# Six pairs of 21 dot products, a turn in the seventh, and additions at other tiles in a one-core transformer block with retrieved experts

## The reference, cut to what matters

```python
def peer(h, w_peer_q, peer_keys, peer_u, peer_v):
    ...
    idx = jnp.take_along_axis(cidx, fpos, axis=-1)
    g = jax.nn.softmax(fv, axis=-1).astype(h.dtype)
    ...
    def block(args):
        xt, it, gt = args
        u = peer_u[it]
        act = jax.nn.gelu(jnp.einsum('thkd,td->thk', u, xt)) * gt
        return jnp.einsum('thk,thkd->td', act, peer_v[it])
```

## Time and profile before

| | us |
|---|---|
| median of 3 runs | 3876.71 (3874.89 to 3881.01) |
| the profiled execution | 3877.76 |
| its span, first to last instruction | 3876.0 |
| PE busy | 3788.0 (98%) |
| DVE busy | 2360.4 (61%) |
| POOL busy | 1769.0 (46%) |
| PE idle before L1702 with act_hi, ended by DVE w_lo | 42.3 |

### The profile page before, as it was taken

One profiled execution on the slowest core, in us unless ns is written; L12 is line 12 of the kernel. 1 busy time (PEld: TensorE's weight loads), 2 busy tenths in 40 slices (PEclk: granted clock), 3 DMA queues, 4 the chain that ended last, 5 costly groups with the idle time before them and its releaser, 6 DMA issues.

```text
span 3876.0 us, 56148 instructions
## 1 busy us (share of the span) xinstructions
PE 3788.0 (98%) x20205; PEld 3470.2 (90%) x20205; DVE 2360.4 (61%) x3821; ACT 1225.9 (32%) x1418; POOL 1769.0 (46%) x1448
## 2 busy tenths in 40 slices
PE   7999999999999999999999999999999999999998
PEld 5778778888888878899999999999999999999998
DVE  5482552001000228887967787878786777888887
ACT  3433453333333223225632222222222222222121
POOL 0444334444444653442015554555553555555544
PEclk9999999999999999999999999999999999999999
DMA  6223212222222332334579998998998889998887
GB/s 204 88 87 104 70 55 98 97 97 97 97 94 93 139 118 86 110 120 166 206 255 337 338 327 325 330 341 322 331 330 298 299 328 337 336 334 324 326 316 272
DMA packets 212719, 836.78 MB, mean 216 GB/s; under 512 B 21264, under 2 KB 84760, under 8 KB 159256
## 3 DMA queue, kind: packets, MB, share of 16 engines
q1 hardware_dynamic: 124608, 528.52, 38.4%
q0 software_dynamic: 83840, 303.09, 21.3%
q10 hardware_dynamic: 4184, 4.01, 0.5%
HBM read 779.43 MB, written 55.05 MB: 215 GB/s over the span
## 4 chain that ended last, share of the span: by engine, by line
PE 81%; DVE 7%; DMA 6%; issue 4%; ACT 1%; POOL 1%; ACTq 0%; DVEq 0%; POOLq 0%
PE bank L1702 80%; DMA grow<-v_rows,g_col 5%; DVE w_lo L1503 2%; DVE g_acc L1581 1%; DMA ring<-w_exp 1%; ACT w_hi L766 1%; POOL grow L735 1%; DVE act_in L1545 1%; DVE ohB L1522 1%; DVE act_hi L1549 0%; DVE xT L1602 0%; DVE ohA L1517 0%; DVE x_acc L1581 0%; DVE act_lo L1551 0%; PE bank L1861 0%
## 5 line engine op out<-in xcount | busy, mean ns | idle before, releaser
L615 POOL TENSOR_TENSOR p_lo<-ring,p_hi 128x512 fp32r<-128x512 f32 x432 | 563.4, 1305 | 673.8 <-ACT p_hi L766 673.8
L766 ACT ACTIVATE w_hi<-ring 128x2048 fp32r<-128x2048 f32 (+1 forms) x275 | 520.8, 1894 | 853.1 <-PE bank L1702 766.8
L1702 PE MATMUL bank<-h_hi,w_hi 128*128 128x368 f32 (+1 forms) x2304 | 779.7, 338 | 8.9 <-DVE h_lo L1409 7.3
L1702 PE MATMUL bank<-h_lo,w_hi 128*128 128x368 f32 (+1 forms) x2304 | 773.8, 336 | 0.0
L1702 PE MATMUL bank<-h_hi,w_lo 128*128 128x368 f32 (+1 forms) x2304 | 773.7, 336 | 0.0
L1702 PE MATMUL bank<-act_hi,w_hi 128*128 128x368 f32 x2048 | 685.7, 335 | 42.3 <-DVE w_lo L1503 42.3
L1702 PE MATMUL bank<-act_lo,w_hi 128*128 128x368 f32 x2048 | 682.1, 333 | 0.0
L1702 PE MATMUL bank<-act_hi,w_lo 128*128 128x368 f32 x2048 | 681.8, 333 | 0.0
L1503 DVE TENSOR_TENSOR w_lo<-ring,w_hi 128x2048 fp32r<-128x2048 f32 x239 | 549.0, 2297 | 191.0 <-ACT w_hi L766 190.8
L735 POOL DMA_INDIRECT grow<-v_rows,g_col x288 | 411.5, 1429 | 446.1 <-DVE g_acc L1581 350.9
L735 POOL DMA_INDIRECT grow<-u_rows,g_col x288 | 407.3, 1414 | 444.0 <-DVE grow L1574 366.1
(11 more groups left out here) (216 smaller groups left out, 5043.7 us busy)
## 6 DMA issues: line engine op xcount, KB each, us to landing
ring<-w_exp SPq DMA_DIRECT2D x256, 1024.0 KB, 6.6
ring<-w_mix SPq DMA_DIRECT2D x64, 1024.0 KB, 5.0
tables<-wt SPq DMA_DIRECT2D x12, 2048.0 KB, 6.8
wg<-tables SPq DMA_DIRECT2D x16, 1536.0 KB, 16.1
gelus<-gel SPq DMA_DIRECT2D x128, 184.0 KB, 5.4
act_in<-gelus SPq DMA_DIRECT2D x16, 1472.0 KB, 14.0
ring<-w_qk SPq DMA_DIRECT2D x20, 1024.0 KB, 5.0
ring<-w_o SPq DMA_DIRECT2D x16, 1024.0 KB, 4.9
```

The lines of the kernel that those rows point to most:

```text
L615: nc.gpsimd.tensor_tensor(p_lo[:, part, :], ring[slot][:, part, :], p_hi[:, part, :].bitcast(F32), ALU.subtract).then_inc(quarter_lo, 1)
L766: return nc.scalar.activation(out, in_, func, **kw)
L1702: return nc.tensor.matmul(out, lhsT, rhs, start=start, stop=stop)
```

## The change

Rows move between the pairs, the turn moves by one pair, and the tail's rows get a table.

```diff
+TAIL_MORE = ((), (0,), (0,), (0, 1, 3, 4, 6))
+TAIL_LESS = ((4, 6), (4, 6), (4, 6), (7,))
-N_DOT = 2 * JG + 4
-N_LOOP = 6
-G_TURN, T_LAST, N_TURN, N_ADD = 7, 4, 13, 2 * JG + 6
-MORE_DOT = (0, 3, 6, 9)
-MORE_ADD = (0, 2, 5, 8, 11, 14)
+MORE_DOT = (1, 4, 7, 9, 15)
+MORE_ADD = (1, 4, 6, 8, 10, 15)
+N_DOT, N_ADD = 2 * JG + len(MORE_DOT), 2 * JG + len(MORE_ADD)
+G_TURN, T_LAST, N_TURN = 6, 13, 2
...
-            def dots(g, q):
+            def dots(side, g, q):
                 i = q + sum(x < q for x in MORE_DOT)
                 for m in range(i, i + 1 + (q in MORE_DOT)):
-                    if isinstance(g, int):
-                        a_u_row(N_DOT * g + m)
-                    else:
-                        dot(N_DOT * g + m, m % 2)
+                    dot(N_DOT * g + m, (N_DOT * side + m) % 2)
...
-                    for i in range(first + (ROWS_U - first) * q // T_LAST, first + (ROWS_U - first) * (q + 1) // T_LAST):
+                    for i in range(first + -(-(ROWS_U - first) * q // T_LAST), first + -(-(ROWS_U - first) * (q + 1) // T_LAST)):
...
-            with dve.Fori(0, N_LOOP) as g:
-                experts(g, dots)
-            for g in range(N_LOOP, G_TURN):
-                experts(g, dots)
+            with dve.Fori(0, G_TURN // 2) as t:
+                for side in range(2):
+                    experts(2 * t + side, partial(dots, side))
...
-                    done = N_TURN + N_ADD * (NG - LAG - G_TURN - 1)
-                    for m in range(done, ROWS_U):
-                        if (m - done) * (JG * LAG - 1) // (ROWS_U - done) == JG * k + q:
+                    for m in range(added_rows, min(added_rows + 1 + (q in TAIL_MORE[k]) - (q in TAIL_LESS[k]), ROWS_U)):
```

More of the change, by code:

```diff
@@ L13 @@
 from contextlib import ExitStack
+from functools import partial
 import concourse.bass as bass
@@ L1668, in _ @@
                 experts(g, added)
+            added_rows = N_TURN + N_ADD * (NG - LAG - G_TURN - 1)
             for k in range(LAG):
@@ L1681, in _ @@
                         weigh(NG - LAG + k + 1, a, 2 * (q - 3) + 1)
-                    done = N_TURN + N_ADD * (NG - LAG - G_TURN - 1)
-                    for m in range(done, ROWS_U):
-                        if (m - done) * (JG * LAG - 1) // (ROWS_U - done) == JG * k + q:
[L1685 to L1688, removed]
+                    for m in range(added_rows, min(added_rows + 1 + (q in TAIL_MORE[k]) - (q in TAIL_LESS[k]), ROWS_U)):
+                        if m < PAIRS:
+                            gather_add(m, m % 2)
+                        else:
+                            x_row_add(m - PAIRS, m % 2)
+                        added_rows = m + 1
+            assert added_rows == ROWS_U
             dve.wait_ge(tail_tr, 1)
```

## The result

The changed kernel takes 3892.91 us (median of 6 runs, 3889.61 to 3899.59), the kernel before beside it 3877.32. The ratio is 1.0041 with a 95% interval of 1.0031 to 1.0051, so it is slower by 0.4%. The forecast was 3860.5, with a range of 3838 to 3882, so the change went the other way than forecast and out of the range.

The account below looks back on a forecast made before the run. PE, busy 98%, bounds the kernel and loses 62.7 us waiting for DVE's late low parts and to the clock; after: 12.5 + 8 + 1 + 18 + 7 = 46.5 lost, 16 won, so 3860.5 us (range 3838 to 3882).

Parts of the forecast that it names:

- Pairs 1 to 5: Pairs of dot products, one more row each: 2.5 us lost a pair (0 to 6), 12.5 in all, nothing before.
- Pairs 8 to 11: Pairs of additions at new places: 4.5 us lost a pair (2.5 to 7), sum 18, against 26.6 before.
- the tail: Last 32 tiles, giving up 11 of 43 rows: 7 us lost (2 to 12) against 36.1 before; wins 29.
- V tile 2 of the dot pairs: Second half row of q = 15 lands at 12.5; low part late by 0.8 us (0 to 2.3).
- surcharge: After a PE wait of some 2.5 us, clock at 0.50 for 3.40 us loses 1.7 us more.
- V tile 4: Dot pairs: second row of q = 1, gathered during the weights' load, makes the low part 1.8 us late (1.3 to 3.8).
- The turn and pair 7: Turn in pair 6: 5.8 us late and the surcharge, 8 lost (3 to 10); pair 7: 1 (0 to 3).
- most of the 7 should be there: Tail's last group, 12 rows in 7 tiles: most of the tail's 7 us loss falls there.
- Rival 2: What the tail wins, the pairs give back: 63 us lost, no change, 3877; chance 0.18.
- Rival 3: DVE late at v tile 2 or 4 of each pair, each wait with the surcharge: 76 us lost, 3890; chance 0.10.
- Rival 4: Each dot product or addition delays the POOL issue beside it by 1.2 us: 12 more, 3872; chance 0.05.
- the rule weighed in the prediction: DVE instruction with two SBUF inputs blocks GpSimd SBUF reads throughout; prediction accepted it for `low`, not dot products (1.2 us later).

Follow-up runs that it names:

- last group: Tail's last group given 3 second rows instead of 5, against the kernel with loop written out and dot row at 11 (3866.40 us): 3861.07 us, ratio 0.9965.

## Why the prediction was wrong, step by step

The step that failed is what the pairs with 21 and 22 rows cost. Pairs 1 to 5 were put at 12.5 us and lost 27.4. Half of that, 14.7, is in pairs 2 and 4, where the loop's jump has no term. Pairs 8 to 11 were put at 18, by their places, and lost 27.5, by the number of their rows; and 5.8 us behind the last tile have no term. The largest term, the tail, was right.

The steps from the changed kernel to the best one, in medians: loop written out 7.7, row at 11 instead of 15 18.8, last group 5.3 (within the intervals), 21 additions 12.9. The forecast missed by 32.4 us; against the profiled execution (3891.25, forecast 3861.5) its terms were too small by 29.7.

- **The loop: no term.** The diff puts two pairs into VectorE's loop body, and the prediction passes over it. 9.7 of the missing microseconds are in pairs 2 and 4, and the run without the loop is 7.7 us shorter (11.8 with the row at 11).
- **V tile 2 of the dot pairs: the path right, its size short.** The second half row of q = 15 was forecast to be used at 12.5 us of the pair, between 11.3 and 14.0; it was used at 11.8, 14.6, 11.3, 11.6 and 13.7 in pairs 2 to 6. With the loop out of the way, pairs 1 to 5 lose 17.7 against 12.5 forecast, and with the row elsewhere 5.1. The 5 us more are the size of the lateness and its surcharge. I took 0.8 and no surcharge. In the changed kernel the waits at v tile 2 were 2.9 us in pair 3 and 2.1 in pair 6, each with 1.7 to 1.9 behind it at the clock of 0.50, as in the earlier trace rows, and almost nothing in pairs 1 and 5. My bound of 2.3 holds the 2.1 and not the 2.9.
- **V tile 4: the lateness right, its cause wrong.** TensorE waits 0.7 to 1.3 us there in pairs 1, 2, 4 and 5 (forecast 1.8). The cause I gave, gathers issued beside the weights' load, fell: with the load gone the waits stayed. What fits the runs is that five rows in three tiles ask for more than two rows' worth of buffers give: with the row of 15 at 11 the waits at v tile 4 are gone. No run shows that on its own.
- **The turn and pair 7: right in size** (6.0 for 8, 0 for 1).
- **Pairs 8 to 11: the wrong model.** Forecast 18, measured 27.5. I took the old 5.3 a pair for a cost of places and let new places win some of it. It was the cost of the 22nd row. The earlier trace rows pointed at it: VectorE idle 80.0 us before additions while it was busy for 108 of 133. I wrote that it stands still for rows that have not landed, but not how often a buffer can go round. Rows enough to ask the question stood in the trace of the kernel before: 22 rows want a round of 11.6 us, and issue and landing alone take 7.3 of it in the mean of pairs 8 to 11, up to 11.5. That 11.6 is too short they do not show; the run with 21 additions does.
- **The tail: right** (9.5 for 7), the largest gain of the sum.
- **Behind the last tile: no term, 5.8 us.** The prediction said that the last group has 12 rows in 7 tiles and that "most of the 7 should be there". What stands behind it, products that wait for the last of these rows and the clock on which they then run, was not looked at.

Rival 2, no change, has a slip: it puts the additions "as now" at 21, but now they lose 26.6, so its own terms make 69 and not 63, 6 us slower than before.

Rival 3, slower by the clock, has the nearest number (3890), with dot pairs 25 (27.4 measured), turn 10 (6.0), additions 28 (27.5), tail 12 (9.5). It was right that the surcharge comes: the granted clock falls to 0.50 in pairs 2, 3, 4, 6, 9, 10 and 11. But landings of 10.6 and 12.0 as the rule, its reason, are not what the trace shows: issue and landing together are 7.4 us in the mean in pairs 1 to 5, 7.5 before. So its number is luck: its size was met by two causes it did not name, the jump and the pace.

Rival 4, a second row that holds POOL back, has no support in its size: the mean issue is 1.4 us, as before. Its mechanism is real, though, and the rule weighed in the prediction was misread. The prediction compared 1.15 us beside a dot product with 2.46 beside `low`. What counts is how long VectorE's instruction still has to run. The first issue ends at 2397.86 and its dot product at 2397.04; the second ends at 2400.63 and its `low` at 2399.80. Both end 0.8 us after VectorE's instruction, so the trace agrees with the rule for both. An issue that begins together with a dot product, in the kernel before (VectorE's row first, then POOL's):

```profile
2410.70 1.22 DVE L1574 SCALAR_TENSOR_TENSOR grow<-grow,h_tok 128x1024 f32<-128x1024 f32 x1
2410.76 1.99 POOL L735 DMA_INDIRECT grow<-u_rows,g_col  x1 [0.31 <-issue]
```

It ends at 2412.75, again 0.8 us after the dot product (2411.92). So a dot product holds an issue back as `low` does, and an addition of a row does too: 234 issues in the kernel before and 229 in the changed one ended in this way behind one of the two. It costs little because most of them begin with only 0.3 to 0.4 us of it left.

What stays open: why single executions of these kernels are up to 23 us apart (3889.47 to 3912.64 with the additions' row at 12), those of the kernel before within 13; what pair 9 loses with 21 additions (4.6 us, seen once); and why the tail loses 24.5 us with 37 rows.

## What to carry to other kernels

Before a row of work is added, count how often its buffers can go round: the time from one issue into a buffer to the next, against the time that the new rate leaves. Here 11.6 us were not enough at any of four sets of places. 12.2 were, at well chosen places: with second rows at 15, at 13 or side by side, 21 rows lost time too. VectorE's busy share of 0.81 did not show it. A single stretch that passes proves little, since it can live on time in hand; look whether the engine falls behind in it. Second rows must stand apart, not beside heavy work of the same engine, and the last ones must not end behind the engine that everything waits for. And a loop body that doubles is a change of its own: look at the engine's instruction packets at the jump, and at what is in hand there.

## What the runs showed of the hardware that I had not expected

- VectorE's jump back over some 500 recorded instructions stops it for 1.75 to 5.27 us (ten jumps in five kernels), each time with two packets of 8192 bytes on queue 14, and VectorE goes on 1.9 to 2.0 us after the first one begins. Over 248 instructions it fetches nothing between 2141.5 and 2840 us, and TensorE loses nothing in these pairs. The trace may put the stall down to another engine (3.93 <-PE) or to "issue" (5.27).
- The stall was free in one kernel (ratio 1.0003) and 11.8 us in another, with the same form of loop.
- An indirect DMA issued on POOL while VectorE is in a dot product or in `low` ends 0.8 us after that instruction does, whatever it has left to run: 1.15 us with 0.33 left, 1.99 with 1.16 left, 2.46 with 1.63 left. Alone it takes 0.95.
- Taking 1.44 MB of 44 a pair from the DMA engines did not make the kernel faster, while one row fewer (1.05 MB) in five pairs, put into the tail, did, by 12.9 us.
- A wait of 2.09 us of TensorE at the end, before 48 short products, is followed by 10.24 us at 0.5 of the clock, where the waits of 2.1 to 4.1 us inside the stream of this kernel are followed by 3.4 or 6.8, or by no fall of the clock at all.
